# Order of work at three seams of a two-layer hybrid decoder step on one core

## The reference

```
a   = rmsnorm(h)
mix = [state mixer(a), attention(a)] @ w_out      # layer 0: S5 and block-sparse; layer 1: HGRN2 and stick-breaking
h   = h + rmsnorm(mix)
u   = rmsnorm(h) @ w_ffn_up;  c = causal conv of width 3 over u
h   = h + rmsnorm((gelu(c_gate) * c_val) @ w_ffn_down)
h   = h + rmsnorm((p @ w_ple_proj) * sigmoid(h @ w_ple_gate))
```

## Time and profile before

| | |
|---|---|
| median of 3 runs | 1949.39 us (1946.25 to 1952.33) |
| the profiled execution | 1946.59 us, its span 1944.8 us |
| PE busy | 1807.3 us, 93% of the span |
| DVE, ACT, POOL busy | 58%, 37%, 2% |
| mean DMA rate | 105 GB/s |
| chain that ended last | PE 81%, DVE 9%, SP's queue 3%, ACT 3%, issue 2%, DMA 1% |

### The profile page before, as it was taken

The page is one execution under the profiler, slowest core; times in us unless marked ns, Lnnn a source line. Parts: engine busy times, 40 slices in busy tenths (PEclk is TensorE's granted clock), DMA queues, the critical chain, the costliest instruction groups (busy, mean ns, idle before and its releaser), DMA issues.

```text
span 1944.8 us, 34321 instructions
## 1 busy us (share of the span) xinstructions
PE 1807.3 (93%) x13384; PEld 1617.6 (83%) x13384; DVE 1125.4 (58%) x2363; ACT 726.3 (37%) x1313; POOL 38.4 (2%) x65
## 2 busy tenths in 40 slices
PE   6899898989999979999999998887989999979997
PEld 5788456989999979988479995445989999979987
DVE  7974465568777652263334865666568777652264
ACT  5323345543233242254323332656543333242252
POOL 1400000000000000000000000000000000000000
PEclk9999788999999989999999996999999999989999
DMA  4133678212222132221031133773212222132211
GB/s 177 66 61 132 212 260 293 87 42 89 87 79 83 41 132 86 78 90 57 21 108 57 55 124 121 265 266 132 88 44 88 87 80 82 41 132 87 77 44 49
DMA packets 77948, 204.13 MB, mean 105 GB/s; under 512 B 12530, under 2 KB 14882, under 8 KB 77314
## 3 DMA queue, kind: packets, MB, share of 16 engines
q1 hardware_dynamic: 75762, 190.36, 29.3%
q0 software_dynamic: 2064, 12.06, 1.8%
HBM read 190.81 MB, written 10.40 MB: 103 GB/s over the span
## 4 chain that ended last, share of the span: by engine, by line
PE 81%; DVE 9%; SPq 3%; ACT 3%; issue 2%; DMA 1%; DVEq 0%; ACTq 0%
PE psum L412 42%; PE psum L585 12%; PE psum L2203 7%; PE psum L2159 4%; PE psum L420 2%; SPq L1312 2%; PE psum L844 1%; PE psum L2352 1%; PE psum L1354 1%; PE psum L507 1%; PE psum L1329 1%; PE psum L521 1%; DVE sb_arena_r L372 1%; DVE sb_ring_r L372 1%; SPq L1296 1%
## 5 line engine op out<-in xcount | busy, mean ns | idle before, releaser
L412 PE MATMUL psum<-sb_a_sb_r,sb_ring_r 128*128 128x288 f32 x1408 | 297.1, 295 | 0.0
L412 PE MATMUL psum<-sb_a_sb_r,sb_arena_r 128*128 128x288 f32 x1344 | 276.5, 296 | 0.0
L412 PE MATMUL psum<-sb_y_sb_r,sb_ring_r 128*128 128x288 f32 x960 | 262.6, 298 | 0.5 <-DVE sb_ring_r L372 0.5
L412 PEld LDWEIGHTS psum<-sb_a_sb_r,sb_ring_r 128*128 128x128 f32 x1408 | 230.9, 188 | 0.4
L412 PEld LDWEIGHTS psum<-sb_a_sb_r,sb_arena_r 128*128 128x128 f32 x1344 | 217.0, 188 | 0.0
L372 DVE TENSOR_TENSOR sb_ring_r<-sb_ring,sb_ring_r 128x1024 fp32r<-128x1024 f32 (+1 forms) x90 | 116.2, 1295 | 169.1 <-ACT sb_ring_r L369 168.1
L412 PE MATMUL psum<-sb_y_sb_r,sb_arena_r 128*128 128x288 f32 x704 | 207.1, 294 | 6.3 <-DVE sb_a_sb_r L372 6.2
L369 ACT ACTIVATE sb_ring_r<-sb_ring 128x1024 fp32r<-128x1024 f32 (+1 forms) x90 | 99.8, 1114 | 300.6 <-PE psum L412 249.3
L412 PEld LDWEIGHTS psum<-sb_y_sb_r,sb_ring_r 128*128 128x128 f32 x960 | 174.9, 189 | 1.6 <-DVE sb_ring_r L372 1.0
L585 PE MATMUL psum<-sb_arena_r 128*128 128x288 f32 x960 | 161.6, 303 | 8.2 <-DVE sb_arena_r L372 8.2
L412 PE MATMUL psum<-sb_arena_r,sb_ring_r 128*128 128x288 f32 x1056 | 146.0, 299 | 20.9 <-DVE sb_arena_r L372 20.9
(11 more groups left out here) (402 smaller groups left out, 3130.2 us busy)
## 6 DMA issues: line engine op xcount, KB each, us to landing
sb_ring<-w SPq DMA_DIRECT2D x166, 512.0 KB, 3.6
sb_ring<-wd SPq DMA_DIRECT2D x32, 704.0 KB, 4.1
sb_arena<-sb_v SPq DMA_DIRECT2D x64, 256.0 KB, 5.5
sb_arena<-moba_v SPq DMA_DIRECT2D x56, 256.0 KB, 6.4
sb_ring<-moba_k SPq DMA_DIRECT2D x32, 256.0 KB, 4.1
sb_a_sb<-moba_k SPq DMA_DIRECT2D x32, 256.0 KB, 5.6
sb_ring<-sb_k SPq DMA_DIRECT2D x32, 256.0 KB, 4.1
sb_a_sb<-sb_k SPq DMA_DIRECT2D x32, 256.0 KB, 5.5
```

The lines of the kernel that those rows point to most:

```text
L412: ins = e.eng.matmul(out[:, half, :], fr(w[p][:, k, :]), fr(x[q][:, k, cols]), start=(first and k == 0 and i == 0), stop=(last and k == kb ...
```

## The change

Three places change their order; no instruction is added or dropped, and no size changes.

1. End of the attention. ACT makes the high part of out slab 0 and of tiles 0 to 3 of `y`, half 0, inside the attention: in layer 0 between the last exponential and the copy of the last transposed unit, in layer 1 after the last unit. It first waits for all sample keys to be used (`k_used`) and all prompt scores to be made. Slab 1's high part stands ahead of the last `copy_out`. DVE makes the low parts of slab 0 and tiles 0 to 3 just ahead of its wait for the last pair's outputs. After the fence, tiles 4 to 7 are split, and then the work goes on as before.
2. `pe_up`. The sum of squares of half 1 stands ahead of the fourth slab's half 0, not behind it.
3. Gate sweep. ACT makes the high parts of slabs 4 and 5 after tiles 3 and 5 of `h`, half 1, not after the first sigmoid. DVE makes their low parts between its update of half 1 and the low parts of `h`. Slabs 6 and 7 keep their place.

```diff
+        def act_out_first(e, layer, scored):
+            e.eng.wait_ge(k_used, NB * (layer + 1))
+            e.eng.wait_ge(scored, 4 * NH)
+            act_slab(e, out_pairs[0], 0)
+            act_split_half(e, y, yh, 0, ks=range(4))
+        def dve_out_first(e):
+            dve_slab(e, out_pairs[0], 0)
+            dve_split_half(e, y, yh, y, 0, ks=range(4))
         def dve_outputs(e, i, n, rden):
             v = e.eng
+            if i == NPAIR - 1:
+                dve_out_first(e)
             v.wait_ge(v_used, 2 * n + 2)
...
                        .then_inc(prob_ready, 1)
+                if u == len(UNITS):
+                    act_out_first(e, 0, sco_ready)
                 if u >= 1:
...
                 if u == len(UNITS):
+                    act_slab(e, out_pairs[1], 1)
                     copy_out(3)
...
                 else:
+                    if j == 3:
+                        pe_squares(e, pair(n0 % 4)[:, 1, :], 1, range(KD)).then_inc(late_norm, 1)
                     mm_half(e, out, split[j], x, 0)
-            pe_squares(e, pair(n0 % 4)[:, 1, :], 1, range(KD)).then_inc(late_norm, 1)
...
-            act_slab(e, out_pairs[0], 0)
-            act_split_half(e, y, yh, 0)
-            for n in range(1, 4):
+            act_split_half(e, y, yh, 0, ks=range(4, KD))
+            for n in range(2, 4):
                 act_slab(e, out_pairs[n], n)
...
-            act_split_half(e, h, hh_, 1, (h_new, e.adds))
+            for k in range(KD):
+                e.eng.wait_ge(h_new, e.adds + k + 1)
+                act_high(e, h[:, k, COLS[1]], hh_[:, k, COLS[1]], xh_ready)
+                if k in (3, 5):
+                    act_slab(e, gate_pairs[4 + (k - 3) // 2], (k - 3) // 2)
+            e.parts += KD
...
                 act_sweep_gate(e, t[f"A{j}"], j, 0)
-                if j < 2:
-                    act_slab(e, gate_pairs[4 + 2 * j], 2 * j)
-                    act_slab(e, gate_pairs[5 + 2 * j], 2 * j + 1)
+                if j == 1:
+                    act_slab(e, gate_pairs[6], 2)
+                    act_slab(e, gate_pairs[7], 3)
                 act_gate_square(e, j, 0)
...
-            dve_slab(e, out_pairs[0], 0)
-            dve_split_half(e, y, yh, y, 0)
+            dve_split_half(e, y, yh, y, 0, ks=range(4, KD))
...
             dve_update(e, layer, "g_ffn_post", 1, rs=False)
+            for n in range(2):
+                dve_slab(e, gate_pairs[4 + n], n)
             dve_split_half(e, h, hh_, hl_, 1)
...
                 if j:
                     dve_part_sum(e, gate_sums[0], 1)
-                dve_slab(e, gate_pairs[4 + 2 * j], 2 * j)
-                dve_slab(e, gate_pairs[5 + 2 * j], 2 * j + 1)
+                    dve_slab(e, gate_pairs[6], 2)
+                    dve_slab(e, gate_pairs[7], 3)
...
+            act_out_first(e, 1, zs_ready)
+            act_slab(e, out_pairs[1], 1)
             copy_out(3)
```

More of the change, by code:

```diff
@@ L562, in dve_pre, with act_split_half @@
                     .then_inc(x_new, 1)
-        def act_split_half(e, src, high, half, after=None):
-            for k in range(KD):
+        def act_split_half(e, src, high, half, after=None, ks=range(KD)):
+            for k in ks:
                 if after is not None:
@@ L569, in act_split_half, with dve_split_half @@
                 act_high(e, src[:, k, COLS[half]], high[:, k, COLS[half]], xh_ready)
-            e.parts += KD
-        def dve_split_half(e, src, high, low, half):
-            for k in range(KD):
+            if KD - 1 in ks:
+                e.parts += KD
+        def dve_split_half(e, src, high, low, half, ks=range(KD)):
+            for k in ks:
                 e.eng.wait_ge(xh_ready, e.parts + k + 1)
                 dve_low(e, src[:, k, COLS[half]], high[:, k, COLS[half]], low[:, k, COLS[half]], xl_ready)
-            e.parts += KD
+            if KD - 1 in ks:
+                e.parts += KD
         def mm_half(e, out, w, x, half, x_parts=None, ks=range(KD)):
```

## The result

The median of 4 runs is 1923.12 us (1921.81 to 1923.87), against 1949.02 us (1946.25 to 1952.33) of 4 runs of the kernel before: the ratio is 0.9866, with a 95% interval of 0.9849 to 0.9883. That is 25.9 us faster. The sum had 19.0 there, so 4.6 of the 7.3 us lie between the two profiles. The other 2.7 lie in the starting value: the profiled execution of before was 2.8 us faster than the median that the sum starts from (1946.59 and 1949.39), that of after only 0.1 us faster than its own (1922.98 and 1923.12).

What follows compares the result with a forecast made beforehand. TensorE (PE), busy 93% of the span, was taken to bound the kernel, so PE's gains at breaks reach the end. 9.5 + 10.4 - 0.9 = 19.0 us off the 1949.39 median gives 1930.4, forecast 1930, range 1925 to 1939.

Steps and rivals of the forecast that it cites:

- The sum: Whole kernel: 9.5 + 10.4 - 0.9 = 19.0 us saved at the three places changed, taken from the median.
- starting value: The 1949.39 us median of the runs shown, from which the 19.0 us was taken to give 1930.4.
- Seam A: End of attention: splits hidden inside it, PE idle 1.1 us in place of 3.98; 9.5 us saved, at least 5.7.
- Seam B: Up projection: square sums 3.18 us sooner, PE idle 1.8 us in place of 4.99; 10.4 us saved, at least 6.4.
- Seam C: Gate sweep: the wait before the fifth slab goes, 4.1 us of idle comes before the seventh; 0.9 us lost.
- The bound of 12: Gate sweep: were the stall gone altogether, 2 x (3.67 + 2.3) = 12 us would be gained.
- The low end of the range: 1925 us: the forecast with 3 us of scatter between runs and a smaller loss in the gate sweep.
- Rival 1: The clock falls at the shorter idles as well, in all four places: sum 11.2 us, time 1938; chance 0.12.
- the clock term: Behind the shortened idles after attention and in the up projection the clock stays up: 3.85 and 4.06 us counted.

Runs made afterwards that it cites:

- the mended kernel: Changed kernel with gate slabs 6 and 7 split before the first sigmoid and product, and squares ahead of the third slab; median 1910.70 us, ratio 0.9822.
- A and B: Changed kernel with the gate sweep left as in the kernel before (parts 1 and 2 only); median 1930.55 us, ratio 0.9918 to the kernel before.
- seam C mended: Changed kernel with gate slabs 6 and 7 split ahead of the first sigmoid (ACT) and first product (DVE); median 1910.36 us, ratio 0.9831.
- before again: The kernel before, unedited, profiled a second time; median 1946.25 us of 10, ratio 0.9997.
- B alone: Only part 2 of the change (sum of squares ahead of the fourth slab) on the kernel before; median 1940.67 us, ratio 0.9951.
- after + 3.0 us: Changed kernel with three and a half extra matmuls at layer 1's input projection; median 1927.24 us, ratio 0.992 to the kernel before.
- A alone: Only part 1 of the change (end of the attention) on the kernel before; median 1934.03 us, ratio 0.9922.
- after + 2.6 us: Changed kernel with three extra matmuls of 512 columns at layer 1's input projection; median 1928.11 us, ratio 0.9889 to the kernel before.
- after again: The changed kernel, unedited, profiled a second time; median 1925.89 us of 4, ratio 0.9894 to the kernel before.
- C alone: Only part 3 of the change (gate sweep) on the kernel before; median 1941.66 us, ratio 0.998.
- before + 0.43: The kernel before with one extra matmul of 256 columns in layer 1's input projection; median 1942.32 us of 12, ratio 0.9997.

## Why the prediction was right in its seams and wrong in its sum

- **Seam A** held in every step: cover of 0.37 and 0.47 us on DVE (0.4 reckoned), idle 1.09 and 0.80 (1.1), clock at 1.00 behind it, 9.4 us (9.5). (ACT is free at 319.19 by the row, not at 319.12; nothing hangs on it.)
- **Seam B** held: idle 1.84 (1.8), the chain moved whole. 9.8 us where 10.4 stood; the 96 matmuls took 13.06 us, not 12.74, at a granted clock of 1.00.
- **Seam C** held: the stall went from the fifth slab to the seventh, 3.84 us (4.1), and cost 0.9 us. The mended order shows that the same seam had 11.3 us to give. (The bound of 12 takes 2.3 us for the slow matmuls; its own row gives 12.10 - 9.55 = 2.55, so 12.4.)
- **The step that failed** is the last sentence of the sum: "Nothing between the seams is tied to a fixed time: loads wait for slots that PE, ACT and DVE free, and all move together." It put every stretch between the seams at no change. The HGRN2 stage came out 8.1 us shorter, through the granted clock: 0.64 before and 0.80 after over the same 60 us of it. The first 328 us came out 2.8 us longer, for the most part through the clock too, and ahead of anything that the change touches. So the profiles differ by 18.3 - 2.8 + 8.1 us. That nothing is tied to a fixed time may still hold for loads; the clock is what the sentence left out. That the clock follows the place of the work in time is argued and not shown. For it stand 8.5 us with one matmul added to before, 7.0 with one added to the mended kernel, and the order of the fourteen profiles given below; but each kernel so moved has one profile, and two of four forecasts of the stage missed. In the nine profiles with seam A the first out sweep starts anywhere from 326.37 to 330.90 us.
- **The starting value** failed as well: the sum takes a difference between profiled executions from a median that lay 2.8 us above the profiled one. After's median lies 0.1 us above its own, and 2.7 of the 7.3 us are that.
- **The low end of the range**, 1925, allowed for 3 us of scatter. With the stage either way it would have had to reach 8 us below the forecast, to 1922, and the measured 1923.12 would lie in it. The forecast itself, 1930, is what the kernel with A and B alone gave, whose stage stayed long (1930.55).
- **Rival 1**, that the clock falls at the shorter idles as well, was not all wrong. In the seven profiles with seam B's idle of 1.84 us it fell behind 5 of the 14 such idles (96 matmuls in 14.57 to 14.60 us) and stayed up behind 9 (13.05 to 13.07). Behind seam A's idles of 1.09 and 0.80 us it fell in 2 of 18 (240 matmuls in 33.42 and 33.43 us, in the kernel with A and B and in the one with seam C mended). Each fall costs about 1.5 us. The Trainium skill, page "TensorE: Matmul & The Clock Gate", section "A second HAM failure mode: psum-queue depth-cycling", says that short idles between groups of matmuls can make the clock swing. This is borne out in part: the lower level came right behind an idle of 0.80 us here, but at most of these idles it did not come. Averaged over these idles the clock term is smaller than I counted, by about 5/14 x 1.5 us at each of seam B's two places and by little at A's.
- **The ground for keeping the clock term** was weak, and that the term came true was in part luck. The prediction argued from one idle, 2.67 us with the clock at 1.00 behind it. At the same place in the profile of after the clock fell (timeline, then a window):

```profile
1318.80 0.49 PE L2670 MATMUL psum<-sb_arena,sb_con 128*128 128x128 f32 x2 [2.67 <-DVE sb_arena L2747]
```

```profile
1318.80:1323.80 5.00, 5.00 (x18) 0.66 0.00 0
```

Eleven of the fourteen profiles have this idle of 2.67 us. In four the clock stayed at 1.00 over the 5 us behind it (before, before again, B alone, after + 3.0 us), in seven it has a mean of 0.66. So an idle of 2.67 us was no proof for shorter ones. That the clock mostly stayed up behind 1.09, 0.80 and 1.84 us is what the counts above show, not what that row could tell.

What stays open: why the fall comes at 172.8 us or ten us of work later. Where it falls parts the fourteen profiles cleanly. In the five long stages it came between 172.76 and 172.88 us and lasted 30.7 us; at 173.07 (A alone) and 173.28 us (after + 2.6 us) it lasted 3.4 us; in the other seven nothing fell before 182.3 us. From the clock's last rise in layer 0's gate sweep to the start of the stage it was 117.3 to 117.4 us in the long ones of before, before again, B alone and A and B; the short ones have 110.9 (after and after again), 111.0 (C alone), 113.4 (after + 2.6), 114.0 (after + 3.0), 117.06 (A alone) and 117.8 (before + 0.43). So tenths of a us seem to part the sides, but my two forecasts from such distances missed. Also open is how often each length comes in executions without a profile, and why the clock in the first 100 us stayed up in some profiles and not in others. The two comparisons of the changed kernel, a gain of 1.3% and of 1.1%, may hold both.

## What to carry to other kernels

Find out before you add up the seams whether a long stage runs at the edge of the clock: a fall in the windows with PE busy throughout, no idle ahead of it, and matmuls of few columns. Here such a stage differed by 7 to 8 us between profiles of kernels that don't differ in it, so it belongs in the range with its own size and in both directions, and a gain or loss found there says nothing about the edit. And when a reordering moves a stall to a later place, read what that place waits for: here one running sum stood ahead of a split that nothing needed it for, and moving the split was worth 12.2 us where the seam's first version had lost 0.9. Last, don't rest the clock behind an idle on one row: look at the same place in a second profile, and count a median from a median and a profile from a profile.

## What the runs showed of the hardware

- The granted clock falls to its lower level (0.50, 1.2 GHz) while PE is busy 8.00 of 8.00 us, in a loop with matmuls of 8 columns: 16 of them take 1.85 us at 1.00 and 3.42 us at 0.50. The last idle of PE ended 7.9 us earlier in before and 17.8 us earlier in after.
- In fourteen profiles the first such fall came at two places only, 172.8 to 173.3 us or 182.3 to 183.0 us into the stage. In the five with the long stage it was the first, and the clock stayed low for some 31 us; in two it was the first and lasted 3.4 us, with the next fall at 183.5 and 186.7 us.
- With one more matmul of 256 columns, 0.43 us, it was at the second place in both kernels whose profile without it had the first (stage 360.26 and 351.71 us, and 357.24 and 350.27 us; one profile each, before two). That the matmul moved it is not shown.
- The mean granted clock of 57 executions of the unchanged kernel before went from 0.954 to 0.967, and their times from 1956.21 down to 1935.45 us.
- An idle of 0.80 us has been followed by the lower level (window of 8 us at 0.79, kernel with seam C mended), one of 1.84 us by the full rate in 9 of 14 cases, and one of 2.67 us at one and the same place by a mean of 0.66 in seven profiles and 1.00 in four.
